# State space heads in pairs: masked decay differences made by TensorE from turned rows

## The reference, cut to what matters

```
a_cs  = cumsum(dt * a)                                # per head, inside a chunk
seg   = a_cs[l] - a_cs[s];  lmat = exp(where(l >= s, seg, -inf))
cb    = C B^T per group
y_diag = (cb * lmat) @ (x * dt)                       # inside the chunk
y_off  = (C * exp(a_cs)) @ state before the chunk
y = y_diag + y_off + x * d;  out = rmsnorm(y * silu(z)) * norm_w
```

## Time and profile before

| what | us |
|---|---|
| median of 3 runs | 1561.8 (1561.37 to 1562.09) |
| the profiled execution | 1564.06 |
| its span | 1562.8 |
| PE busy | 1454.9 (93%) |
| DVE busy | 1024.0 (66%) |
| ACT busy | 760.2 (49%) |
| POOL busy | 122.1 (8%) |
| stage of the heads, first row matmul to the norm's sum | 262.4 to 328.8 |

### The profile page before, as it was taken

How to read it: one execution, slowest core, us unless ns; L and a number is a source line. 1 busy time by engine, 2 the same in 40 slices (tenths; PEclk the granted TensorE clock), 3 DMA queues, 4 the chain that set the end, 5 groups by cost and what they waited for, 6 DMA issues and landing times.

```text
span 1562.8 us, 17703 instructions
## 1 busy us (share of the span) xinstructions
PE 1454.9 (93%) x6975; PEld 1163.5 (74%) x6975; DVE 1024.0 (66%) x1361; ACT 760.2 (49%) x999; POOL 122.1 (8%) x148
## 2 busy tenths in 40 slices
PE   7899989889989999999999999899999799999981
PEld 5777658668767788888888788787658688888871
DVE  4888885555435565446546657865555798988976
ACT  5453354644434422222224543235564788887863
POOL 0500000000000000000000303300000111111012
PEclk9989999999999999999999999999999899999996
DMA  5212223203112342233223231111005699999975
GB/s 210 77 68 81 81 92 120 87 1 108 60 48 81 135 148 82 86 130 108 73 74 110 82 108 54 55 55 55 28 1 202 269 396 425 407 422 412 411 297 188
DMA packets 39330, 231.58 MB, mean 148 GB/s; under 512 B 4400, under 2 KB 5696, under 8 KB 17104
## 3 DMA queue, kind: packets, MB, share of 16 engines
q1 hardware_dynamic: 30640, 200.09, 33.9%
q0 software_dynamic: 7648, 27.87, 4.8%
q10 hardware_dynamic: 960, 2.49, 0.4%
HBM read 213.66 MB, written 16.78 MB: 147 GB/s over the span
## 4 chain that ended last, share of the span: by engine, by line
PE 74%; DVE 13%; ACT 6%; issue 4%; DMA 2%; POOL 0%; POOLq 0%; ACTq 0%; DVEq 0%
PE bank L457 14%; PE bank L458 14%; PE bank L459 14%; PE bank L3035 5%; PE bank L3037 5%; PE bank L3036 5%; PE bank L603 3%; DVE w_lo L384 2%; PE bank L476 1%; ACT w_hi L378 1%; PE bank L477 1%; PE bank L478 1%; PE bank L2264 1%; PE bank L2285 1%; PE bank L843 1%
## 5 line engine op out<-in xcount | busy, mean ns | idle before, releaser
L457 PE MATMUL bank<-h_hi,w_hi 128*128 128x512 f32 x952 | 384.4, 404 | 11.4 <-DVE w_lo L384 8.5
L458 PE MATMUL bank<-h_lo,w_hi 128*128 128x512 f32 x952 | 374.2, 393 | 0.0
L459 PE MATMUL bank<-h_hi,w_lo 128*128 128x512 f32 x952 | 373.9, 393 | 0.0
L384 DVE TENSOR_TENSOR w_lo<-w_raw,w_hi 128x2048 fp32r<-128x2048 f32 (+3 forms) x86 | 188.2, 2188 | 90.6 <-ACT w_hi L378 90.0
L457 PEld LDWEIGHTS bank<-h_hi,w_hi 128*128 128x128 f32 x952 | 181.0, 190 | 60.6 <-DVE w_lo L384 11.7
L459 PEld LDWEIGHTS bank<-h_hi,w_lo 128*128 128x128 f32 x952 | 180.7, 190 | 38.9
L458 PEld LDWEIGHTS bank<-h_lo,w_hi 128*128 128x128 f32 x952 | 181.1, 190 | 37.5 <-issue 2.2
L378 ACT ACTIVATE w_hi<-w_raw 128x2048 fp32r<-128x2048 f32 (+3 forms) x87 | 154.7, 1778 | 61.7 <-PE bank L459 61.7
L3220 DVE TENSOR_TENSOR h_lo<-w_raw,h_hi 128x2048 fp32r<-128x2048 f32 x32 | 73.2, 2291 | 12.3 <-ACT h_hi L3121 10.4
L3220 DVE TENSOR_TENSOR lo_b<-raw_b,hi_b 128x2048 fp32r<-128x2048 f32 x32 | 73.1, 2285 | 5.9 <-ACT hi_b L3121 5.9
L457 PE MATMUL bank<-a_hi,w_hi 128*128 128x512 f32 x176 | 68.5, 389 | 0.0
(11 more groups left out here) (592 smaller groups left out, 2813.3 us busy)
## 6 DMA issues: line engine op xcount, KB each, us to landing
w_raw<-in_params_dram SPq DMA_DIRECT2D x122, 1024.0 KB, 4.9
raw_b<-in_params_dram SPq DMA_DIRECT2D x51, 1024.0 KB, 7.9
w_raw<-in_params_dram SPq DMA_DIRECT2D x16, 704.0 KB, 4.0
result_rows<-osb POOLq DMA_DIRECT2D x16, 512.0 KB, 8.4
result_rows<-prm POOLq DMA_DIRECT2D x8, 512.0 KB, 3.2
xt<-in_x_t_dram POOLq DMA_DIRECT2D x1, 2048.0 KB, 9.3
scratch_rows<-htm SPq DMA_DIRECT2D x4, 512.0 KB, 2.9
out_dram<-pr SPq DMA_DIRECT2D x4, 512.0 KB, 2.6
```

Source lines behind the costliest of these rows:

```text
L384: V.tensor_tensor(k.w_lo[g % SPLIT][:, 0:size], k.raw[:, g % RAW, 0:size], k.w_hi[g % SPLIT][:, 0:size].bitcast(F32), ALU.subtract).then_i ...
L457: PE.matmul(ps, wh, hi[:, c, 0:width], start=c == 0, stop=False)
L458: PE.matmul(ps, wh, lo[:, c, 0:width], start=False, stop=False)
L459: m = PE.matmul(ps, wl, hi[:, c, 0:width], start=False, stop=c == parts - 1)
```

## The change

Heads go through TensorE in pairs, two heads' matmuls in turn, on two halves of the output channels. `lm` and `ce` get a second buffer each (four heads in flight). The difference is no longer made by ScalarE: TensorE adds, in bank 5, a mask (identity times a tile with -1e30 where it is masked) and the difference itself (one matmul over turned rows that hold both row and column parts), so that ScalarE takes one exponential of bank 4 to `ce` and one of bank 5 to `lm`. Both banks are now single: the next head's row waits for the exponential before. The cumulated sums are split in two float32r parts, turned in one piece of 96 rows and one of 24. GpSimd makes the constant rows, and for each head `decay_of` (the turned columns times a selector); it no longer masks `cb`. The squares are taken one pair later. In `pe_s5_in` and `act_s5_step` the loops over part and group change places.

```diff
-        jj, part = n // 2, n % 2
+        part, jj = n // 2, n % 2
         r0 = 32 * ((2 * q + jj) % 4)
...
-    for t in range(TT):
-        G.wait_ge(s.sd_cbt, t + 1)
-        x = k.cbt[:, :, t, :]
-        pool_select(k, x, x, ALU.is_ge, 0.0, 0, [[0, SSD_G], [1, P]], -1).then_inc(s.sd_tri, 1)
...
+    k.g(G.memset(exact, -1.0))
...
+    k.g(pool_select(k, chunks, exact, ALU.is_ge, 0.0, 0, [[-n, TT], [0, P]], 1))
...
+    k.g(pool_select(k, chunks, exact, ALU.is_ge, 0.0, n - 1, [[n, TT], [0, P]], -1))
+    G.wait_ge(s.m_mul, DB)
+    k.g.own()
+    G.memset(k.decay[:, :], 1.0).then_inc(s.sd_decay, 1)
+    G.wait_ge(s.sd_dve, 7)
+    for h in range(SSD_H):
+        if h >= 2:
+            G.wait_ge(s.sd_row, 2 * h - 2)
+        G.tensor_scalar(k.decay_of[:, h % 2, :], k.decay[:, :], k.head_of[:, h:h + 1], None, ALU.mult).then_inc(s.sd_decay, 1)
...
-            if h >= 2:
-                PE.wait_ge(s.sd_lexp, h - 1)
-            PE.matmul(k.bank[4 + h % 2][:, :], k.ident[0:SSD_H, h:h + 1].broadcast_to([SSD_H, P]), k.afm, start=True, stop=True).then_inc(s.sd_row, 1)
+            if h:
+                PE.wait_ge(s.sd_exp, 2 * h - 1)
+            PE.matmul(k.bank[4][:, :], k.row_of[:, h:h + 1].broadcast_to([P, P]), k.afm[:, :], start=True, stop=True).then_inc(s.sd_row, 1)
+            if h:
+                PE.wait_ge(s.sd_exp, 2 * h)
+            PE.matmul(k.bank[5][:, :].rearrange("p (t l) -> p t l", t=TT), k.ident_r[:, :],
+                      k.later[:, :].rearrange("p (o l) -> p o l", o=1).broadcast_to([P, TT, P]), start=True, stop=False)
+            PE.wait_ge(s.sd_decay, h + 2)
+            PE.matmul(k.bank[5][:, :], k.decay_of[:, h % 2, :], k.afm[:, :], start=False, stop=True).then_inc(s.sd_row, 1)
...
+        if step >= 3 and step % 2:
+            pe_ssd_pair(k, (step - 3) // 2)
...
+    PE.wait_ge(s.sd_ce, 2 * blk + 2)
+    if blk >= 2:
+        PE.wait_ge(s.sd_z, blk - 1)
...
+    for t in range(TT):
+        at = slice(t * P, t * P + P)
+        for i in range(2):
+            h = 2 * blk + i
+            m = PE.matmul(out[HD * i:HD * i + HD, at], k.xdt[:, t, h * HD:h * HD + HD], lm[:, i, t, :],
+                          start=t == 0, stop=t == 0, skip_group_check=True)
+        if t:
+            for i in range(2):
+                h = 2 * blk + i
+                m = PE.matmul(out[HD * i:HD * i + HD, at], k.S[:, t - 1, h * HD:h * HD + HD], ce[:, i, t, :],
+                              start=False, stop=True, skip_group_check=True)
...
-        if h >= 2:
-            A.wait_ge(s.sd_out, h - 1)
-        ps = k.bank[4 + h % 2][:, :].rearrange("p (t l) -> p t l", t=TT)
-        a(A.activation(k.ce[:, i, :, :], ps, ACT.Exp))
-        for t in range(TT):
-            a(A.activation(k.lm[:, i, t, :], ps[:, t, :], ACT.Relu, bias=acs[:, t, h:h + 1], scale=-1.0))
-        a.own()
-        A.activation(k.lm[:, i, :, :], k.lm[:, i, :, :], ACT.Exp, scale=-1.0).then_inc(s.sd_lexp, 1)
+        if h >= 4 and not i:
+            A.wait_ge(s.sd_out, h // 2 - 1)
+        A.activation(ce[:, i, :, :], k.bank[4][:, :].rearrange("p (t l) -> p t l", t=TT), ACT.Exp).then_inc(s.sd_exp, 1)
+        A.wait_ge(s.sd_row, 2 * h + 2)
+        A.activation(lm[:, i, :, :], k.bank[5][:, :].rearrange("p (t l) -> p t l", t=TT), ACT.Exp).then_inc(s.sd_exp, 1)
...
+    v(V.tensor_copy(da.bitcast(F32R), acs))
+    v(V.tensor_tensor(k.row_of[:, :], k.ident[:, TURNED:TURNED + SSD_H], k.ident[:, TURNED + SSD_H:TURNED + 2 * SSD_H], ALU.add))
+    v(V.tensor_reduce(k.head_of[:, :], k.ident[:, 0:TURNED + 2 * SSD_H].rearrange("p (j h) -> p h j", h=SSD_H), AX.X, ALU.add))
+    v.own()
+    V.tensor_tensor(d.bitcast(F32R), acs, da, ALU.subtract).then_inc(s.sd_dve, 1)
...
-    V.tensor_copy(k.afm, k.bank[7][0:SSD_H, :]).then_inc(s.sd_dve, 1)
+    V.wait_ge(s.sd_decay, 1)
+    v(V.tensor_copy(k.ident_r[:, :], k.ident[:, :]))
+    v(V.tensor_scalar(k.later[:, :], k.tri[:, :], 1.0, -SMALL, ALU.subtract, ALU.mult))
+    v(V.tensor_copy(k.decay[0:TURNED, :], k.bank[7][0:TURNED, 0:P]))
+    v.own()
+    V.tensor_copy(k.afm[TURNED:TURNED + 2 * SSD_H, :], k.bank[7][TURNED:TURNED + 2 * SSD_H, :]).then_inc(s.sd_dve, 1)
...
-        if h >= 7 and h % 2:
-            dve_add_square(k, "ssd", k.xbc, (h - 5) // 2, T)
+        if h >= 9 and h % 2:
+            dve_add_square(k, "ssd", k.xbc, (h - 7) // 2, T)
```

More of the change, by code:

```diff
@@ L218, in __init__ @@
         base = m.at
-        self.rs, self.dtr = m("rs", [P, T]), m("dtr", [P, TT, SSD_H])
+        rs_at = m.at
+        self.rs = m("rs", [P, T])
+        dtr_at = m.at
+        self.dtr = m("dtr", [P, TT, SSD_H])
         m.line()
@@ L242, in __init__ @@
         self.S, self.xdt, self.btm = m("S", [P, TT - 1, SSD_W]), m("xdt", [P, TT, SSD_W]), m("btm", [P, TT, T])
+        self.ident_r, self.later = m("ident_r", [P, P], F32R), m("later", [P, P], F32R)
         self.cbt = self.xbc[:, 6:10, :].rearrange("p g (t l) -> p g t l", t=TT)
@@ L245, in __init__ @@
         self.ncb = self.prm[:, a:a + 256].rearrange("p (j c) -> p j c", j=8)
-        self.afm = self.prm[0:SSD_H, a:a + T]
+        self.afm = Memory(nc, (prm_at + 4 * a + 31) // 32 * 32)("afm", [P, T], F32R)
+        x = Memory(nc, dtr_at)
+        self.row_of, self.head_of = x("row_of", [P, SSD_H], F32R), x("head_of", [P, SSD_H])
+        x = Memory(nc, rs_at)
+        self.decay, self.decay_of = x("decay", [P, P]), x("decay_of", [P, 2, P], F32R)
+        self.lm = (self.lm, Memory(nc, h_at + 2 * T * 4)("lm1", [P, 2, TT, P]))
+        self.ce = (self.ce, Memory(nc, h_at + (DB + 2) * T * 4)("ce1", [P, 2, TT, P]))
         self.sq0 = self.xbc[:, 0:DB, :]
@@ L866, in act_s5_step @@
             A.wait_ge(s.s5_rot, 4 * q)
-        A.activation(k.bu[:, n % 2, n // 2, :], k.bank[4 + n % 2][:, :], ACT.Copy).then_inc(s.s5_buc, 1)
+        A.activation(k.bu[:, n // 2, n % 2, :], k.bank[4 + n % 2][:, :], ACT.Copy).then_inc(s.s5_buc, 1)
         if q == 3:
@@ L1148, in ssd_small, with ssd_both @@
 def ssd_small(k):
-    return [k.sm[:, i, :, :] for i in range(6)]
+    dt, acs, e1, u = (k.sm[:, i, :, :] for i in (0, 5, 3, 4))
+    both = ssd_both(k)
+    return dt, both[:, :, 0:SSD_H], acs, e1, u, both[:, :, SSD_H:2 * SSD_H]
+TURNED = 2 * SSD_H * TT
+def ssd_both(k):
+    return k.sm[:, 1:3, :, :].rearrange("p i t h -> p (i t h)").rearrange("p (t x) -> p t x", t=TT)
 def act_ssd_steps(k):
@@ L1223, in pe_ssd @@
     PE.wait_ge(s.s5_skip, 2)
-    PE.wait_ge(s.sd_dve, 4)
+    PE.wait_ge(s.sd_dve, 5)
     for t in range(TT):
-        m = pe_turn(k, k.bank[7][0:SSD_H, t * P:t * P + P], acs[:, t, :])
+        PE.matmul(k.bank[7][TURNED:TURNED + 2 * SSD_H, t * P:t * P + P], ssd_both(k)[:, t, :], k.ident[:, :], start=True, stop=True, tile_position=(0, TURNED))
+    m = pe_turn(k, k.bank[7][0:TURNED, 0:P], ssd_both(k).rearrange("p t x -> p (t x)"))
     m.then_inc(s.sd_pe, 1)
     PE.wait_ge(s.silu, XBC_B)
-    PE.wait_ge(s.sd_dve, 6)
+    PE.wait_ge(s.sd_dve, 7)
     PE.wait_ge(s.s5_sig, 2)
@@ new lines, in pe_ssd_pair @@
+def pe_ssd_pair(k, blk):
+    PE, s = k.nc.tensor, k.s
+    PE.wait_ge(s.sd_ce, 2 * blk + 2)
+    if blk >= 2:
+        PE.wait_ge(s.sd_z, blk - 1)
+    lm, ce = k.lm[blk % 2], k.ce[blk % 2]
+    out = k.bank[6 + blk % 2]
+    for t in range(TT):
[9 more added lines that the diff above has]
+                              start=False, stop=True, skip_group_check=True)
+    m.then_inc(s.sd_out, 1)
@@ L1296, in act_ssd @@
     act_s5_glu(k)
-    A.wait_ge(s.sd_dve, 5)
+    A.wait_ge(s.sd_dve, 6)
     a(A.activation(e1, e1, ACT.Exp))
@@ L1324, in act_ssd @@
             act_split_to(k, SLOT0["w_out"] + 1)
-        if h >= 3 and h % 2:
-            ssd_square(k, (h - 3) // 2)
+        if h >= 5 and h % 2:
+            ssd_square(k, (h - 5) // 2)
+    ssd_square(k, 4)
     ssd_square(k, 5)
@@ L1385, in dve_ssd @@
                 V.tensor_copy(x, ps).then_inc(s.sd_S, 1)
-    V.wait_ge(s.sd_tri, 4)
+    V.wait_ge(s.sd_cbt, 4)
     for h in range(SSD_H):
         i, blk = h % 2, h // 2
[L1389 to L1392, removed]
+        lm, ce = k.lm[blk % 2][:, i, :, :], k.ce[blk % 2][:, i, :, :]
+        V.wait_ge(s.sd_exp, 2 * h + 1)
+        v(V.tensor_tensor(ce, ce, k.xbc[:, 10 + h // HPG, :].rearrange("p (t l) -> p t l", t=TT), ALU.mult))
+        V.wait_ge(s.sd_exp, 2 * h + 2)
+        v.own()
+        V.tensor_tensor(lm, lm, k.cbt[:, h // HPG, :, :], ALU.mult).then_inc(s.sd_ce, 1)
         if h + EARLY_VALUES < DB:
```

31 lines of the change are left out of this document (13 added, 18 removed).

## The result

The changed kernel takes 1543.46 us (median of 4 runs, 1541.46 to 1545.91), beside 1561.94 us for the kernel before (4 runs, 1561.37 to 1568.71). The ratio is 0.9864, with a 95% interval of 0.9838 to 0.9891: 1.4% faster. The forecast was 1545.0 in a range of 1538 to 1554. The profiled execution took 1541.83 us, its span 1540.5.

What follows compares the result with a forecast made beforehand. Bound by TensorE (93% busy), in the heads' second half by ScalarE and VectorE. Stage -16.9, set-up +1.2, other mixer -1.0: net -16.7 from 1564.06 gives 1547.4, median 1545; range 1538 to 1554.

Steps and rivals of the forecast that it cites:

- TensorE's rows: Per head, three float32r matmuls at 0.23 us replace one plain float32 row matmul of 1.05: 0.69 us.
- Pairs: Outputs of two heads in alternating column halves overlap two to one: 1.7 us a pair, 3.34 before.
- the rival that the halves don't overlap: Outputs of two heads cost 3.1 us; the stage schedule gives 50.6, +4.1, so 1549 us; chance 0.16.
- A step with a value block: Steps 0 to 5 of the heads, set by TensorE: 0.69 + 3.07 = 3.76 us each; row 6 at 25.9.
- VectorE's list: After row 6 of the heads, VectorE's work sets the pace; norm at 46.5 us from the first row.
- the two surcharges: Added to the stage's 46.5 us: 1.0 for GpSimd holding VectorE up, 2.0 for TensorE's lower clock.
- GpSimd's port: Each `decay_of` holds VectorE up by up to 0.29 us: +1.0 in the head loop, +0.55 in the set-up.
- The rival of the port stalls: `decay_of` waits behind 2.2 us VectorE splits, TensorE behind it: two or three 2 us stalls, 1550 us; chance 0.06.
- Clock: Gaps of 2 to 3 us before pairs 4 and 5 lower TensorE's clock at the stage's end: +2.0 us.
- Set-up: Before the heads, three small instructions (0.65 us) and the first two `decay_of` (0.55) on the chain: +1.2 us.
- Other mixer: Neighbouring products on different rows overlap, giving 0.4 to 0.6 us in three of four places: -1.0 us.
- Sum: Stage 49.5 against 66.4 us (-16.9), set-up +1.2, other mixer -1.0: net -16.7 us.

## Why the prediction was right, step by step

- **TensorE's rows** (0.69 forecast): 3 x 0.23 = 0.69. Right.
- **Pairs** (1.7): 1.68. Where neighbours share a half, 2.82, and 1.68 for each single head (3.1 forecast for two). Right; the rival that the halves don't overlap is refuted by the pair in the changed kernel's chain and by the kernel with the halves in turn.
- **A step with a value block** (3.76): 3.57, since the block takes 2.88 behind the float32r matmuls and took 3.07 before. Row 6 came at 25.2, not 25.9.
- **VectorE's list** (46.5 without the two surcharges): 46.9. Gate 1 was to start at 26.1 and started at 25.3; gates 2 to 5 were to end at 34.1, 38.0, 42.4 and 45.0 and ended at 33.7, 37.9, 42.6 and 45.4. The list ran up to 0.8 us early and ended 0.4 late. It lost that in what it did not have: VectorE's wait for itself, 0.19 us a head, and a little by the two squares of 0.64 on the chain. That VectorE sets the end, and not ScalarE, is shown by the changed kernel's chain; with the old exponentials ScalarE comes back onto it.
- **GpSimd's port** (+1.0 in the stage, +0.55 in the set-up): nothing on VectorE. This term failed. From one pair of rows in which a VectorE instruction had waited I made a rule on who waits. Here GpSimd waits (0.60 becomes 2.12), VectorE stays at 0.69, and tripling `decay_of` makes TensorE wait. The price of 0.29 was too low as well: `decay_of` takes 0.60 undisturbed. The rival of the port stalls had the right victim, TensorE, but its stalls come only with three times the work.
- **Clock** (+2.0): nothing in the stage of the profiled execution; 1.00 throughout. The gap in front of the last pair is there as forecast (2 to 3 us; it is 3.04), and what I said would follow it did not. It did in six other kernels, with gaps of 2.42 to 3.35 us. Two of them have the very stage of the changed kernel, and they show what the term is worth: 47.5 and 47.3 us for 46.9, 0.4 to 0.6 and not 2.0. So the mechanism is real in most executions seen, the size was three times too large or more, and that it was missing here was luck. The lower clock appeared ahead of the stage instead, where I had no term for it: the state products, 2.93 for 1.57.
- **Set-up** (+1.2): +0.74. The small instructions cost 0.65 in sum as forecast, `h_lo` 1.29 for 1.20, and GpSimd's selects were over in time.
- **Other mixer** (-1.0): -2.5 in the traces, 3.0 by the kernel with the order put back. The mechanism was right and the size was off: I had counted 0.4 to 0.6 us in three of four places, and the products' busy time fell by a third (18.1 to 11.7 us in 32 instructions). By the chains of waits the second and third places brought 0.3 and 0.6, the last nothing. The first alone brought 1.6: its second set of products took 3.40 us at a clock of 0.56 before and 1.61 at 1.00 now. I had no term for the clock there.
- **Sum.** The stage 49.5 forecast, 46.9 measured: both surcharges failed, 3.0 together. The set-up was 0.5 cheaper and the mixer gave 1.5 more than forecast, and the stretch in front of the stage ate 1.6 of it. The profiled execution came at 1541.83 for 1547.4, with 2.6 us of the difference in later code. The medians moved by 18.5 where the sum said 16.7. That the forecast lies only 1.5 us from the median is in part luck: in the traces the saving was 5.5 us larger than forecast, and the profiled execution of the changed kernel was 1.6 below its median, that of the kernel before 2.1 above.

What stays open: why the state products fell to the lower clock in this execution, and why the last pair did not. The one trace of the kernel that lacks only VectorE's own wait did not keep the clock in its last pair. An estimate from its list (last product through at 40.4) and the 5.6 us that follow at the upper clock, as in the kernel with the transposes, gives 46.0 for the stage, 0.9 less than the changed kernel and near the 1.1 expected.

## What to carry to other kernels

When a stage runs in lock step, draw the circle through buffers and queues before you count work: the cheaper exponentials alone gave 4.6 of 66.4 us, and 11.2 more once second buffers opened the circle. Place small matmuls so that neighbours use other columns or rows of the array. Before you move work to fill a wait, look whether another engine is full and needs that work early, as VectorE was in the other mixer. And when a cut moves the bound to another engine, look at that engine's own small waits and at the gap that it leaves on TensorE, before you expect the next microsecond.

## What the runs showed of the hardware

- A float32r matmul of 512 columns runs at 0.23 us also with a broadcast weight (`row_of`) or a broadcast moving side (`later`); the plain float32 one with a broadcast weight took 1.05.
- GpSimd's 128x128 `tensor_scalar` took 0.60 us undisturbed and 1.53 to 2.16 beside VectorE's work, and VectorE's 128x512 multiplication kept a mean of 0.69 us beside it (0.76 at most); in the earlier trace rows it was the other way round.
- Two sets of 14 matmuls of 128 columns by 64 took 1.68 us in alternating halves, 2.82 when only the end of one met the start of the other.
- Gaps of 2.42 to 3.35 us in front of the last pair were followed by the lower clock in six kernels, with steps of 0.43 for 0.22; one of 3.04 us in the changed kernel was not (1.00). With 0.31 to 0.66 us idle there, once because of 20 transposes, three kernels kept the upper level.
- Behind a gap of 2.22 to 2.23 us in thirteen traces, the same eight state products ran at the upper clock in eight (1.57 us), at the lower in two (2.93), and took 2.1 to 2.4 in three.
